# A fused two-block kernel: the conditioning vectors' products and sums on GpSimd instead of VectorE

## The reference

```python
mod = jax.nn.silu(c) @ w_ada[layer] + b_ada[layer]          # (1, 6 * 1024)
sh1, sc1, g1, sh2, sc2, g2 = jnp.split(mod[:, None, :], 6, axis=-1)
mod_c = jax.nn.silu(c_ctx) @ w_ada[layer] + b_ada[layer]
...
hx = modulate(rms_norm(x, norm1_gain[layer]), sh1, sc1)
x = x + g1 * mixer_output(...)
```

```python
def _swiglu(h, w_in, w_out):
    a, b = jnp.split(h @ w_in, 2, axis=-1)
    return (jax.nn.silu(a) * b) @ w_out
```

## Time and profile before

| | |
|---|---|
| median of 3 runs | 2810.62 us (2810.45 to 2811.58) |
| span of the profiled execution | 2809.6 us |
| PE busy | 2789.2 us, 99% |
| DVE busy | 1480.9 us, 53% |
| ACT busy | 1004.1 us, 36% |
| POOL busy | 39.4 us, 1% |

### The profile page before, as it was taken

One profiled execution on the slowest core, in us unless ns is written; L12 is line 12 of the kernel. 1 busy time (PEld: TensorE's weight loads), 2 busy tenths in 40 slices (PEclk: granted clock), 3 DMA queues, 4 the chain that ended last, 5 costly groups with the idle time before them and its releaser, 6 DMA issues. The chain is left out here.

```text
span 2809.6 us, 34071 instructions
## 1 busy us (share of the span) xinstructions
PE 2789.2 (99%) x13596; PEld 2316.1 (82%) x13596; DVE 1480.9 (53%) x2014; ACT 1004.1 (36%) x1159; POOL 39.4 (1%) x77
## 2 busy tenths in 40 slices
PE   9999999999999999999999999999999999999998
PEld 7888887788888888888877888888898988888888
DVE  7774357457753477533665444435555543633333
ACT  4222237432222322223555322324544432422222
POOL 0000000000000000000000000000000000000000
PEclk9999999999999999999999999999999999999999
DMA  5432231134422234223111322224322122222222
GB/s 177 153 136 99 96 136 61 45 120 142 149 106 105 105 141 150 105 105 108 52 54 61 120 90 105 90 105 149 113 76 70 46 82 99 91 90 94 101 104 77
DMA packets 69040, 288.27 MB, mean 103 GB/s; under 512 B 7680, under 2 KB 30336, under 8 KB 40528
## 3 DMA queue, kind: packets, MB, share of 16 engines
q1 hardware_dynamic: 60480, 257.18, 25.8%
q0 software_dynamic: 8032, 29.37, 3.0%
q10 hardware_dynamic: 432, 0.36, 0.1%
HBM read 284.78 MB, written 2.10 MB: 102 GB/s over the span
## 5 line engine op out<-in xcount | busy, mean ns | idle before, releaser
L1248 DVE TENSOR_TENSOR sb_WL<-sb_RAW,sb_WH 128x2048 fp32r<-128x2048 f32 x240 | 549.8, 2291 | 745.8 <-ACT sb_WH L515 745.8
L2196 PE MATMUL PS<-sb_HH,sb_WH 128*128 128x512 f32 (+1 forms) x2304 | 901.4, 391 | 4.7 <-DVE sb_HL L1264 2.0
L2198 PE MATMUL PS<-sb_HH,sb_WL 128*128 128x512 f32 (+1 forms) x2304 | 894.0, 388 | 0.0
L2197 PE MATMUL PS<-sb_HL,sb_WH 128*128 128x512 f32 (+1 forms) x2304 | 893.7, 388 | 0.0
L515 ACT ACTIVATE sb_WH<-sb_RAW 128x2048 fp32r<-128x2048 f32 x239 | 457.4, 1914 | 792.7 <-PE PS L2198 792.1
L2196 PEld LDWEIGHTS PS<-sb_HH,sb_WH 128*128 128x128 f32 x2304 | 432.9, 188 | 98.7 <-issue 5.9
L2197 PEld LDWEIGHTS PS<-sb_HL,sb_WH 128*128 128x128 f32 x2304 | 433.0, 188 | 90.3 <-issue 2.4
L2198 PEld LDWEIGHTS PS<-sb_HH,sb_WL 128*128 128x128 f32 x2304 | 432.8, 188 | 89.5
L2196 PE MATMUL PS<-ff_GH,sb_WH 128*128 128x512 f32 (+1 forms) x924 | 350.5, 379 | 0.0
L2198 PE MATMUL PS<-ff_GH,sb_WL 128*128 128x512 f32 (+1 forms) x924 | 350.1, 379 | 0.0
L2197 PE MATMUL PS<-ff_GL,sb_WH 128*128 128x512 f32 (+1 forms) x924 | 350.1, 379 | 0.0
(11 more groups left out here) (397 smaller groups left out, 2504.5 us busy)
## 6 DMA issues: line engine op xcount, KB each, us to landing
sb_RAW<-in_weights SPq DMA_DIRECT2D x221, 1024.0 KB, 4.8
ff_ADAW<-in_w_ada POOLq DMA_DIRECT2D x48, 512.0 KB, 3.9
sb_RAW<-in_weights SPq DMA_DIRECT2D x39, 512.0 KB, 4.8
out_t<-sb_XT SPq DMA_DIRECT2D x8, 256.0 KB, 2.4
sb_XT<-in_x SPq DMA_DIRECT2D x3, 512.0 KB, 8.7
sb_RAW<-in_weights SPq DMA_DIRECT2D x4, 256.0 KB, 4.0
b_CT<-in_ctx POOLq DMA_DIRECT2D x1, 1024.0 KB, 4.9
hy_BD<-in_c_gates POOLq DMA_DIRECT2D x1, 512.0 KB, 3.5
```

The source lines that it names most:

```text
L1248: dve.tensor_tensor(WL[slot][:, :], RAW[slot][:, :], f32(WH[slot][:, :]), ALU.subtract).then_inc(*T["w_lo"].up())
L2196: pe.matmul(out, wh, xh, start=start, stop=False)
L2197: pe.matmul(out, wh, xl, start=False, stop=False)
L2198: return pe.matmul(out, wl, xh, start=False, stop=stop)
```

## The change

POOL does the products and sums of the conditioning itself, behind each half that it loads. The fused multiply-add becomes two instructions: a multiply into PROD (256 columns of a hole in the layout), and an add of PROD to ACC. A unit has 30 counted steps instead of 16: 16 multiplies and 14 adds, each of 128 x 256 fp32. POOL's loop over units is written out. DVE keeps the transpose and the reduction, which wait for 30 steps a unit, and loses its `conditioning`. POOL waits for `cond_ready` before its first load; DVE no longer does.

```diff
@@ -178,6 +178,7 @@
 
         ff = layout("ff", [("GH", [P, FT, S], F32R), ("GL", [P, FT, S], F32R), ("ADAW", [P, 1024], F32), ("ACC", [P, 2, UC], F32),
                            ("HOLE", [P, 416], F32), ("ADAR", [P, ADA_PER, 16], F32), ("FOLD", [P, 32], F32)])
+        PROD = ff["HOLE"][:, 0:UC]
         GH, GL, ADAW, ACC, ADAR, FOLD = ff["GH"], ff["GL"], ff["ADAW"], ff["ACC"], ff["ADAR"], ff["FOLD"]
         hy = layout("hy", [("GT", [P, 4, S], F32), ("Q", [P, 4, S], F32), ("K", [P, 4, S], F32), ("V", [P, TB, 512], F32),
                            ("XC", [P, 4, S], F32), ("R", [P, 4, S], F32), ("I", [P, 4, S], F32), ("CH", [P, S], F32R),
@@ -443,24 +444,36 @@
 
             def conditioning(f):
 
-                def half(u, h):
+                def half(i, h):
+                    u = i + ADA_PER * f
+                    if h or i or f:
+                        pool.wait_ge(T["ada_step"].sem, 30 * i + (30 * ADA_PER * f + 14 * h))
                     pool.dma_start(ADAW[:, :], A["w_ada"][u, :, 1024 * h:1024 * h + 1024]).then_inc(*T["ada_in"].up(16))
-
-                if f:
-                    pool.wait_ge(T["ada_step"].sem, 16 * ADA_PER * f)
-                half(ADA_PER * f, 0)
-                with pool.Fori(0, ADA_PER - 1) as i:
-                    pool.wait_ge(T["ada_step"].sem, 16 * i + (16 * ADA_PER * f + 8))
-                    half(i + ADA_PER * f, 1)
-                    pool.wait_ge(T["ada_step"].sem, 16 * i + (16 * ADA_PER * f + 16))
-                    half(i + (ADA_PER * f + 1), 0)
-                pool.wait_ge(T["ada_step"].sem, 16 * ADA_PER * (f + 1) - 8)
-                half(ADA_PER * (f + 1) - 1, 1)
+                    pool.wait_ge(T["ada_in"].sem, 32 * i + (32 * ADA_PER * f + 16 * h + 16))
+                    for k in range(4 * h, 4 * h + 4):
+                        for j in range(2):
+                            w, c = ADAW[:, UC * (k % 4):UC * (k % 4) + UC], CS[:, 2 * k + j:2 * k + j + 1]
+                            if k == 0:
+                                if i or f:
+                                    pool.wait_ge(T["ada_turn"].sem, u)
+                                ins = pool.tensor_scalar(ACC[:, j, :], w, c, None, ALU.mult)
+                            else:
+                                done = 30 * ADA_PER * f + 4 * k + 2 * j - 2
+                                pool.wait_ge(T["ada_step"].sem, 30 * i + done)
+                                pool.tensor_scalar(PROD, w, c, None, ALU.mult).then_inc(T["ada_step"].sem, 1)
+                                pool.wait_ge(T["ada_step"].sem, 30 * i + (done + 1))
+                                ins = pool.tensor_tensor(ACC[:, j, :], ACC[:, j, :], PROD, ALU.add)
+                            ins.then_inc(T["ada_step"].sem, 1)
+
+                for i in range(ADA_PER):
+                    half(i, 0)
+                    half(i, 1)
 
             pool.wait_ge(x_in[2], 16)
             for dst, name in ((ONES, "c_ones"), (IDENT, "c_ident"), (CEX, "c_cex")):
                 pool.dma_start(dst[:, :], A[name]).then_inc(*T["small_in"].up(16))
             pool.wait_ge(raw_loaded[1], 16)
+            pool.wait_ge(T["cond_ready"].sem, 1)
             conditioning(0)
             pool.wait_ge(T["ada_mod"].sem, 1)
             pool.wait_ge(T["visit_done"].sem, U_HY)
@@ -1384,24 +1397,9 @@
                                              RCOL[:, t0 + t:t0 + t + 1], None, ALU.mult)
                 return last
 
-            def conditioning(u, h):
-
-                dve.wait_ge(T["ada_in"].sem, 32 * u + 16 * h + 16)
-                for k in range(4 * h, 4 * h + 4):
-                    for j in range(2):
-                        w, c = ADAW[:, UC * (k % 4):UC * (k % 4) + UC], CS[:, 2 * k + j:2 * k + j + 1]
-                        if k == 0:
-                            if not isinstance(u, int) or u > 0:
-                                dve.wait_ge(T["ada_turn"].sem, u)
-                            ins = dve.tensor_scalar(ACC[:, j, :], w, c, None, ALU.mult)
-                        else:
-                            dve.wait_ge(T["ada_step"].sem, 16 * u + (2 * k + j - 1))
-                            ins = dve.scalar_tensor_tensor(ACC[:, j, :], w, c, ACC[:, j, :], ALU.mult, ALU.add)
-                        ins.then_inc(T["ada_step"].sem, 1)
-
             def turned_sums(i, base):
 
-                dve.wait_ge(T["ada_step"].sem, 16 * i + (16 * base + 16))
+                dve.wait_ge(T["ada_step"].sem, 30 * i + (30 * base + 30))
                 dve.transpose(PS[:, 7, :], ACC[:, :, :].rearrange("p j c -> p (j c)")).then_inc(T["ada_turn"].sem, 1)
                 dve.wait_ge(T["ada_turn"].sem, i + (base + 1))
                 dve.tensor_reduce(ADAR[:, i - 1, :], PS[:, 7, :].rearrange("p (b r) -> p b r", r=32), AX, ALU.add).then_inc(T["ada_sum"].sem, 1)
@@ -1457,14 +1455,11 @@
                         split_at(u0, 2, i, 2)
                         scaled(i, first)
                         rest()
-                    if carry:
-                        conditioning(i + (ADA_PER * n - 1), 0)
                     if not first or not rest:
                         split_at(u0, 2, i, 2)
                         if late:
                             scaled(i, first)
                     if carry:
-                        conditioning(i + (ADA_PER * n - 1), 1)
                         turned_sums(i, ADA_PER * n - 1)
 
                 carries = n < N_ADA // ADA_PER
@@ -1586,7 +1581,6 @@
                 step(dve.tensor_tensor(FOLD[:, :], FOLD[:, :], IDENT[:, 64:96], ALU.add))
                 dve.tensor_tensor(FOLD[:, :], FOLD[:, :], IDENT[:, 96:128], ALU.add).then_inc(*T["fold_ready"].up())
                 dve.tensor_copy(col("ml_b", 1, rows=100)[64:100, :], col("ml_b", 1, rows=36)).then_inc(*T["mlb_in"].up())
-                dve.wait_ge(T["cond_ready"].sem, 1)
 
             ffn(0, lead=start_sums, rest=start_small)
```

## The result

The changed kernel takes 3189.39 us (median of 4, 3188.7 to 3191.49), the kernel before, measured along with it, 2811.07. The ratio is 1.1345, 95% interval 1.1332 to 1.1359: 378 us slower. I had predicted 3040, range 2935 to 3150. The direction and the place were right, the size was not.

What follows compares the result with a forecast made beforehand. PE's matmuls were taken to bound the kernel. Adds 11.8, multiplies 9.6, loads 8.2 and locks 4.1 made a POOL unit of 33.7 us, delaying the three FFNs by 229.9 us: 3040 us, range 2935 to 3150.

Steps and rivals of the forecast that it cites:

- 16 multiplies with wake-up: POOL's multiplies in a unit, each taken as 0.5 us plus 0.1 us to wake from the instruction before: 9.6 us.
- 2 loads: POOL's two loads a unit, each 3.9 us from issue to landing plus 0.2 us for wake-ups: 8.2 us.
- locks: POOL held up in each unit by DVE instructions with two SBUF inputs: 4.1 us.
- Rival (b): POOL's multiply costs as much as the add, wake-ups 0.17 us: 3176 us, or 3128 with wake-ups of 0.1; chance 0.13.
- T: Time of one conditioning unit on POOL, a serial chain: 33.7 us forecast, against PE's 21.76 us a pair.
- 23T - 545: Total delay over the three conditioning FFNs, T being the unit's time on POOL: 229.9 us at T = 33.7.
- 8T - 179.2: Delay of the first FFN from its eight POOL units of T us each, forecast near 90 us.
- Rival (d): PE's clock falls during its stops; at full size all conditioning pairs run at 1.2 GHz: 3332 us; chance 0.04.
- Rival (a): No lock of weight between POOL and DVE, so 4.1 us a unit vanish: T = 29.6, 2946 us; chance 0.10.
- exclusive lock of the prediction: Pair shared by DVE and POOL, held for a whole instruction by two-SBUF-input DVE or any GpSimd operation; 4.1 us a unit.
- Rival (c): POOL's unit stays hidden in the conditioning FFNs, at lowest T = 21.5: 2810 to 2811 us; chance 0.03.
- Rival (e): DVE's lighter queue lets PE run on, gaining at most 2 us; chance of over 0.2% faster 0.01.

Runs made afterwards that it cites:

- e1: Changed kernel with POOL's 16 multiplies a unit taking a constant 0.5 instead of the scalar per partition; 3143.06 us.
- e2: Changed kernel with POOL's multiply written as a two-input instruction, CS broadcast along the columns, same numbers; 3076.05 us.
- e5: Changed kernel without POOL's 14 adds a unit, the products going straight to ACC; 2919.49 us.
- e10: Changed kernel with 15 extra PE matmuls into an unused bank, ahead of PE's wait for the low part in pairs 2 to 9; 3187.43 us.
- e9: Changed kernel with POOL doing only the second condition, in quarter loads, and the first left out; 2810.64 us.

## Why the prediction was wrong

**What bounds it: right.** PE was the bound, DVE's relief bought nothing, and POOL's serial chain became the longest in the conditioning stages.

**The step that failed: the multiply.** I took 0.5 us, between a memset (0.15) and the add (0.74). It takes 0.92. It lies outside my bounds, since I let the two-input form bound the one-input form. The terms of the unit:

| term | predicted | measured |
|---|---|---|
| 14 adds with wake-up | 11.8 | 14 x 0.82 = 11.5 |
| 16 multiplies with wake-up | 9.6 | 16 x 1.01 = 16.2 |
| 2 loads | 8.2 | 2 x 4.4 = 8.8 |
| locks | 4.1 | the rest, 3.2 |
| unit | 33.7 | 39.7 |

The multiplies are 6.6 us longer than predicted, the three other terms together 0.6 shorter. At 23 us of time for each, the multiplies alone are 152 us, about the 149 by which the prediction was off. e1 and e2 change this term alone, and e5 shows what a microsecond of the unit is worth. Rival (b), a multiply as dear as the add with wake-ups of 0.17, gave T = 39.6 and 3176 us. Its time was close, but by other terms: the wake-up is 0.08 to 0.10, and the multiply is dearer than the add. I gave it 0.13.

**The line 23T - 545: right in slope, some microseconds short.** With T = 39.68 it gives 367, measured 378. The first FFN is late by 140.5 us (POOL's first instruction behind it starts at 512.10, before at 371.57); 8T - 179.2 gives 138.2. Part of what is missing is the clock. PE's timeline in the changed kernel around the last pause of that FFN:

```profile
340.34 0.39 PE L2192 MATMUL PS<-sb_HH,sb_WL 128*128 128x512 f32 x1
356.15 0.76 PE L2190 MATMUL PS<-sb_HH,sb_WH 128*128 128x512 f32 x1 [15.43 <-DVE sb_SQT L1442]
356.72 0.63 PE L2191 MATMUL PS<-sb_HL,sb_WH 128*128 128x512 f32 x1
357.14 0.63 PE L2192 MATMUL PS<-sb_HH,sb_WL 128*128 128x512 f32 x1
```

Before the pause matmuls started 0.23 us apart, behind it 0.43. The stretches that follow (busy us, granted clock, DMA share, GB/s):

```profile
356.00:360.00 4.00, 3.85 (x9) 0.50 0.48 203
360.00:364.00 4.00, 4.00 (x14) 0.74 0.32 86
364.00:380.00 16.00, 16.00 (x78) 1.00 0.30 111
```

Matmuls start 0.43 us apart from 356.15 to 361.84 here; behind the last pause of the second FFN they do so from 1058.33 to 1061.84, of the third from 1532.23 to 1536.20. Behind e10's pause in the third FFN the second matmul started 0.31 us after the first and the next ones 0.23 apart. Against that, the 13, 8 and 9 slow starts cost 2.6 + 1.6 + 1.8 = 6.0 of the 11 us. For the third FFN e10 bears it out: it gave 1.9 us back there. I had reckoned the fall hidden in the pause. Behind every pause but the last of an FFN there is another pause to take it up: PE's busy time grew by 50.3 us in all, the end of the kernel is some 6 us later for it. Behind the last there is none.

The rest is mostly the first unit of the second FFN, by these lines of POOL's and DVE's timelines:

```profile
730.12 0.54 POOL L451 DMA_DIRECT2D ff_ADAW<-in_w_ada  x1 [215.36 <-PE PS L2192]
734.18 4.37 POOL L459 TENSOR_SCALAR ff_ACC<-ff_ADAW,sb_CS 128x256 f32<-128x256 f32 x2 [3.52 <-DMA ff_ADAW<-in_w_ada]
...
774.90 0.73 DVE L1403 STREAM_TRANSPOSE PS<-ff_ACC 128x512 f32<-128x512 f32 x1 [5.96 <-POOL ff_ACC L465]
```

It takes 44.8 us from its load to its transpose, 5.1 more than T, since POOL meets more of DVE's work there: its first two multiplies alone took 4.37 us instead of 1.85. The other seven units of that FFN take 39.6 each.

Rival (d) at full size did not come: behind the last stop of an FFN the clock was back after 3.5 to 5.7 us. By the rule of the Trainium skill (TensorE: Matmul & The Clock Gate, Why this matters for your kernels), that idle gaps send the clock back, the trace agrees: 0.50 behind a pause of 15.4 us.

**The locks: 3.2 us for 4.1, and one-sided.** Rival (a), none, fell: the multiply at 120.78 took 3.36 us. Counted directly, by what the means of POOL's multiplies and adds lie above their undisturbed durations, it is 3.5 us a unit. But DVE's low part was to be stretched above 2.29 us where it begins during a POOL instruction, and behind a one-input multiply it was not. First the changed kernel, the low part that began 0.37 us into that multiply; then e2, with a two-input multiply:

```profile
121.15 2.28 DVE L1261 TENSOR_TENSOR sb_WL<-sb_RAW,sb_WH 128x2048 fp32r<-128x2048 f32 x1
...
214.10 0.94 POOL L470 TENSOR_TENSOR ff_HOLE<-ff_ADAW,sb_CS 128x256 f32<-128x256 f32 x1
214.49 2.70 DVE L1270 TENSOR_TENSOR sb_WL<-sb_RAW,sb_WH 128x2048 fp32r<-128x2048 f32 x1
```

In the changed kernel 22 low parts began during a POOL multiply, and 21 of them took 2.28 or 2.29 us. The trace so agrees only in part with the exclusive lock of the prediction: it was POOL's multiply that was held up, though it had begun first.

**Rival (c)** fell, but e9 shows what it rests on: under PE's pair nothing is paid. **Rival (e)** was not to be seen; even e9, with less work on DVE, is no faster than before.

The Trainium skill (GPSIMD Engine Reference, 4.1 Engine selection) says of one-input operations that they run at roughly line rate, against two-input ones that are about twice as slow as on VectorE. Here the trace does not agree: the one-input multiply of 256 columns took 0.92 us, against 0.35 on DVE; on POOL the two-input form took 0.61 with a broadcast operand and 0.74, as an add, with two full tiles. The measurement decides.

## What to carry to other kernels

An engine that is 1% busy is not free capacity: ask for the length of the chain that it would run serially, issue, landing, wake-ups and locks included, and hold it against the period of the work that it has to keep up with. Below that period the work cost nothing here, above it each microsecond was paid about once per round. Do not bound an unmeasured form of an instruction by another form of the same engine; give the upper end more room, or measure the form alone first. When two engines share a buffer, a load behind a wait in an in-order queue holds up all work queued behind it.

## What the runs showed of the hardware that I had not expected

On GpSimd, for 128x256 fp32: a multiply by a scalar per partition took 0.92 us, by a constant 0.85, and by the same scalar as a broadcast second operand 0.61; an add of two tiles took 0.74. An instruction that waits for the one before it on its own engine starts 0.08 to 0.10 us after it; one that waits two back starts at once. A one-input GpSimd multiply met by DVE's low part of 2.28 us took up to 3.37 us, though it had begun first, and the low part took its 2.28; beside a two-input GpSimd multiply the low part took 2.70. Behind PE pauses of 14.8 to 15.4 us the clock was at its lower level (0.50 granted, matmuls 0.43 us apart) for 3.5 to 5.7 us; behind a pause of 2.4 us matmuls started 0.23 us apart at once.
